# Moving the first head's projections into the last state-space group, and the first merge tiles' products and modulation terms into the last head

## What is computed

```python
hl = rms_norm(xl, g_pre_mix) * (1.0 + sc1_l) + sh1_l        # latent; hc the same for the context
z, xbc, dtr, q, f, i, og, gm, gh = split(h @ w_in)          # one input projection
xbc = silu(dwconv_centred(xbc, conv_w, conv_b))
y  = ssd_scan(...) + xs * d_skip                            # state-space branch: 4 groups of 8 heads, 2 directions
o  = gla_scan(silu(q), k(f), i, log_f)                      # gated linear attention (HGRN2): 8 heads, 2 directions
ys = rms_norm(ys * silu(z), g_ssm_norm)
oh = rms_norm(oh, g_hg_norm) * silu(og)
mixed = sigmoid(gm) * (ys @ w_branch_ssm) + sigmoid(gh) * (oh @ w_branch_hg)
xl = xl + gt1_l * rms_norm(mixed @ w_out, g_post_mix)
hl = rms_norm(xl, g_pre_ffn) * (1.0 + sc2_l) + sh2_l        # mod = silu(c) @ w_ada + b_ada gives sh, sc, gt
xl = xl + gt2_l * rms_norm(hier_moe(hl), g_post_ffn)        # 32 experts, top 2 inside the top group
```

## Time and profile before

| | us |
|---|---|
| median of 3 runs | 2322.83 (2321.36 to 2323.81) |
| the profiled execution, its own time | 2327.91 |
| its span | 2326.1 |
| PE busy | 1916.5 (82%) |
| DVE busy | 829.7 (36%) |
| ACT busy | 512.8 (22%) |
| POOL busy | 360.4 (15%) |

### The profile page before, as it was taken

How to read it: one execution, slowest core, us unless ns; L and a number is a source line. 1 busy time by engine, 2 the same in 40 slices (tenths; PEclk the granted TensorE clock), 3 DMA queues, 4 the chain that set the end, 5 groups by cost and what they waited for, 6 DMA issues and landing times.

```text
span 2326.1 us, 20169 instructions
## 1 busy us (share of the span) xinstructions
PE 1916.5 (82%) x7320; PEld 1043.9 (45%) x7320; DVE 829.7 (36%) x1438; ACT 512.8 (22%) x781; POOL 360.4 (15%) x400
## 2 busy tenths in 40 slices
PE   6888888888885898899988679999964977778773
PEld 2454544544543566666656544444442333333321
DVE  1444354444456065554566442212232000000003
ACT  2221231231322144433244320000240000000002
POOL 1011011021020144323444310000000100000000
PEclk9898898998996899999999799999976999999996
DMA  6113113103111211111110136242336999999993
GB/s 242 40 36 95 44 33 91 45 27 99 36 37 36 81 46 36 36 36 36 36 45 9 45 143 209 94 150 81 112 139 267 428 430 430 429 429 429 429 418 134
DMA packets 153549, 350.16 MB, mean 151 GB/s; under 512 B 14066, under 2 KB 104395, under 8 KB 140443
## 3 DMA queue, kind: packets, MB, share of 16 engines
q1 hardware_dynamic: 144282, 332.68, 37.9%
q10 hardware_dynamic: 4176, 8.41, 1.0%
q0 software_dynamic: 5040, 8.40, 1.0%
HBM read 346.09 MB, written 13.32 MB: 155 GB/s over the span
## 4 chain that ended last, share of the span: by engine, by line
PE 59%; DMA 17%; DVE 9%; issue 7%; ACT 6%; POOL 2%; SPq 1%; DVEq 0%; ACTq 0%; POOLq 0%
PE bank L575 11%; PE bank L1066 7%; PE bank L1045 5%; PE bank L1865 5%; DMA arena<-in_w_up_dram 4%; PE bank L1386 4%; PE bank L629 4%; PE bank L1071 3%; DMA arena<-in_w_down_dram 3%; DMA arena<-in_w_gate_dram 3%; PE bank L1405 2%; PE bank L647 2%; PE bank L1883 2%; PE bank L1390 2%; PE bank L1104 2%
## 5 line engine op out<-in xcount | busy, mean ns | idle before, releaser
L575 PE MATMUL bank<-stay,arena 128*128 128x512 f32 (+1 forms) x704 | 253.9, 521 | 24.8 <-DVE arena L732 22.6
L1865 PE MATMUL bank<-arena 128*64 128x512 f32 x832 | 201.8, 642 | 52.5 <-DMA arena<-in_w_up_dram 33.3
L575 PEld LDWEIGHTS bank<-stay,arena 128*128 128x128 f32 x704 | 140.6, 201 | 143.3 <-issue 117.9
L1066 PE MATMUL bank<-arena 128*128 128x512 f32 x384 | 180.4, 625 | 20.0 <-ACT arena L973 15.8
L1865 PEld LDWEIGHTS bank<-arena 128*64 128x64 f32 x832 | 70.4, 148 | 182.3 <-issue 179.1
L1927 DVE TENSOR_TENSOR arena<-arena,bank 128x512 f32<-128x512 f32 x17 | 11.7, 688 | 331.2 <-PE bank L1865 331.2
L1066 PEld LDWEIGHTS bank<-arena 128*128 128x128 f32 x384 | 76.5, 203 | 113.3 <-issue 91.5
L629 PE MATMUL bank<-arena,stay 128*128 128x512 f32 x256 | 120.9, 628 | 0.0
L1045 PE MATMUL bank<-stay,arena 128*128 128x512 f32 x256 | 116.1, 612 | 0.0
L1386 PE MATMUL bank<-stay,arena 128*128 128x512 f32 x256 | 111.2, 592 | 0.0
L1104 PE MATMUL bank<-arena 128*128 128x128 f32 x448 | 68.7, 306 | 49.1 <-DVE arena L1212 36.2
(11 more groups left out here) (370 smaller groups left out, 2838.4 us busy)
## 6 DMA issues: line engine op xcount, KB each, us to landing
arena<-in_w_gate_dram SPq DMA_DIRECT2D x26, 2048.0 KB, 26.4
arena<-in_w_up_dram SPq DMA_DIRECT2D x26, 2048.0 KB, 27.6
arena<-in_w_down_dram SPq DMA_DIRECT2D x24, 2048.0 KB, 27.0
arena<-in_w_in_dram SPq DMA_DIRECT2D x64, 512.0 KB, 4.0
arena<-in_w_ada_dram SPq DMA_DIRECT2D x12, 2048.0 KB, 10.1
stay<-in_w_down_dram SPq DMA_DIRECT2D x10, 2048.0 KB, 26.4
stay<-in_w_gate_dram SPq DMA_DIRECT2D x8, 2048.0 KB, 26.6
stay<-in_w_up_dram SPq DMA_DIRECT2D x8, 2048.0 KB, 27.4
```

What stands on the lines that cost most here:

```text
L575: mm = pe.matmul(ps[:, 0:n], w[:, k, :], hT[:, k, o:o + n], start=(k == 0), stop=(k == KT - 1))
L1066: mm = pe.matmul(b[:, :], w[:, k, :], src[:, k, 0:LAT], start=(k == 0), stop=(k == KT - 1))
L1865: mm = pe.matmul(b[cols, :], xgT[r][:, k, cols], w[u][:, k, :], start=(k == 0), stop=(k == KT - 1))
```

## The change

Three things are moved, and nothing is computed otherwise:

1. `unit` and `unit_copy` become `head_unit` and `head_unit_copy`, and head 0's eight units stand in the last group at the places where the other groups have `project`: units 0 and 1 at `j` = 8, 2 and 3 at 10, 4 at 12, 5 at `q` = 1, 6 at `q` = 3, 7 behind the last `q`. Their copies stand on ScalarE at `j` = 9, 11, 13, behind the z gate's SiLU, and behind the norm. The weights of head 0 are loaded behind the row of head 1 of the last group. The arena is laid out anew so that weights and projected values lie where nothing of the last group is alive.
2. In the last head, TensorE does the gate products of tiles 0 and 1 (copied out raw by `gate_copy`, their sigmoid taken in place later), and the state-space product of tile 0 in four quarters. What stays of tile 0 behind the head is the product with `ohT`; of tile 1 the two branch products.
3. The `w_ada` tile of tile 0 is loaded as soon as the head's units let go of `hTp`, and VectorE takes its eight operations in the last head, between the chunk states and the end of the head.

The mask wait of VectorE (`s_lev`) stands behind the first head's start. Other edits (one memset semaphore fewer, a shared one for the output norm, a strided home for the gates in `hT`) move nothing.

```diff
+        def early_gate(pe, j, b, half):
+            if not half:
+                if j:
+                    pe.wait_ge(s_wm[1], 32)
+                    pe.wait_ge(s_gc, b + 1)
+                else:
+                    pe.wait_ge(s_wg1, 32)
+                    pe.wait_ge(s_pev, START + 8 * HH - 1 + b)
+            for k in range(4 * half, 4 * half + 4):
+                mm = pe.matmul(bank[b][:, :], wmg[j][:, 8 * b + k, :], hT[:, k, 0:LAT], start=(k == 0), stop=(k == KT - 1))
+            if half:
+                mm.then_inc(s_gmp, 1)
+        def early_ssm(pe, quarter):
+            if not quarter:
+                pe.wait_ge(s_wm[0], 32)
+                pe.wait_ge(s_gc, 3)
+            for k in range(4 * quarter, 4 * quarter + 4):
+                pe.matmul(bank[0][:, :], wmb[0][:, k, :], ysT[:, k, :], start=(k == 0), stop=(k == 15))
...
+                    if last and j in (8, 10, 12):
+                        if j == 8:
+                            pe.wait_ge(s_hp, KT)
+                        for u in {8: (0, 1), 10: (2, 3), 12: (4,)}[j]:
+                            head_unit(pe, 0, u)
...
+                    if last and q in (1, 3):
+                        head_unit(pe, 0, 5 + q // 2)
...
+                else:
+                    head_unit(pe, 0, 7)
...
                 if not last:
                     for u in range(4):
-                        unit(h + 1, u)
+                        head_unit(pe, h + 1, u)
+                else:
+                    for b in range(2):
+                        for half in range(2):
+                            early_gate(pe, 0, b, half)
...
-                    if last and i in (0, 2):
-                        if i == 0:
-                            pe.wait_ge(s_pev, START + 8 * HH)
-                        pe.wait_ge(s_wm[0], 64)
-                        merge_gate(pe, i // 2, 0)
+                    if last and i == 0:
+                        early_gate(pe, 1, 0, 1)
+                    if last and i in (2, 3):
+                        early_gate(pe, 1, 1, i - 2)
+                    if last and i in (4, 5):
+                        early_ssm(pe, i - 4)
...
                 if not last:
-                    unit(h + 1, 7)
+                    head_unit(pe, h + 1, 7)
+                else:
+                    early_ssm(pe, 2)
                 pe.wait_ge(s_sqh, h + 1)
                 pe.matmul(bank[7][:, :], ones[:, :], sqb, start=True, stop=True).then_inc(s_sum, 1)
+                if last:
+                    early_ssm(pe, 3)
...
                 if not last:
                     start(h + 1)
                     sums(h + 1)
+                else:
+                    modulation_terms(dve, own, 0)
                 finish(h)
```

More of the change, by code:

```diff
@@ L521, in body @@
                         centre(g + 1, (j - 9) // 2, False)
+                    if last and j in (9, 11, 13):
+                        for u in {9: (0, 1), 11: (2, 3), 13: (4,)}[j]:
+                            head_unit_copy(act, 0, u)
                 act.wait_ge(s_zc, 4 * g + 4)
@@ L825, in ssd_vector @@
             body(G - 1, True)
-        at[0] = after_long
-        wh = [take(KT, P) for _ in range(5)]
+        at[0] = KT * LAT
         pf = [take(T) for _ in range(2)]
         pq, pog, pV = take(LAT), take(LAT), take(T)
+        Vh = take(NCH, P)
+        assert at[0] == after_long
+        wh = [take(KT, P) for _ in range(5)]
+        ohT = take(KT, LAT)
+        after_oh = at[0]
         lf = [take(T) for _ in range(2)]
@@ L851, in build @@
         lbh, omlh, ghg = take(2), take(2), take(1)
+        KD = [take(T) for _ in range(2)]
         NL = len(LEVELS)
@@ L1074, in hg_tensor @@
-            for u in range(8):
-                unit(0, u)
             def body(h, last):
```

268 lines of the change are left out of this document (159 added, 109 removed).

## The result

The changed kernel takes 2271.25 us in the median of 4 runs (2264.99 to 2273.61), the kernel before, on the same chip, 2323.32 (2321.36 to 2329.52): a ratio of 0.9767, 95% interval 0.9753 to 0.9781, or 54 us saved (51 to 57). The forecast was 56.0 us, 2266.8.

The account below looks back on a forecast made before the run. The closing expert-weight stream, DMA-bound, starts only after the second norm, so savings ahead of it count in full: 29.6 (units less masks) plus 26.4 (last head, merge tiles) gave 56.0 us, 2266.8 from 2322.83, range 2254 to 2284.

Parts of the forecast that it names:

- Units, 30.0 said: Last group: head 0's units cost 21.3 us there and free the 51.3 us they held alone, gaining 30.0.
- The rival by which the units hide nothing: Last group: inserted units lengthen each step, gain 3.8 us instead of 29.6, giving 2292.6; chance 0.06.
- Masks, 0.4 late said: Head 0's start: GpSimd's masks end at 795.2, its first head work is due at 794.8, so 0.4 us late.
- the rival's text: Masks beside VectorE's scans slowed 2.2 times, 13.4 us late, 2280.2; about 2 us called more probable; chance 0.06.
- the sign of being right: Head 0's start: the masks were to end within 1 us of the first scan.
- The last head, +4.3 said: Last head: gate and state-space pieces put into TensorE's queue end the head 4.3 us later.
- half a product (3.5): Last head, behind level 2: half a gate product on TensorE was put at 3.5 us.
- the rival of the pieces at the lower clock: Last head: six pieces between levels and behind outputs take 7 us, not 3.5; 21 us more, 2287.8; chance 0.08.
- Terms and merge tiles: Behind the last head: tiles 0 and 1 need 30.0 us instead of 60.7; modulation operations hidden in the head.
- The 26.4: Last head and merge tiles together: 30.7 us gained behind the head less 4.3 for its later end.
- The stream's length: End of program: the expert weights' stream does not depend on its start, so savings ahead arrive in full.
- The clock staying low through the merge tiles: Merge tiles: each loses 36 us at the lower clock, 2483 with all six; chance 0.02 of slower than before.

Follow-up runs that it names:

- units_alone: Changed kernel with head 0's eight units back in a row ahead of the loop over heads, weights still loaded early: 2292.75 us, ratio 0.985.
- masks_early: Changed kernel with head 0's level masks in a tensor of their own, made without waiting for the last group's transposes: 2272.85 us, ratio 0.9772.
- gaps_masks: Changed kernel with last-head pieces set into earlier gaps, tile 1's whole first gate ahead of level 0, and masks in their own tensor: 2256.19 us, ratio 0.9695.
- gaps_masks_2: The kernel of `gaps_masks` run once more, beside the same kernel without the masks' own tensor: 2260.77 us, ratio 0.9705.
- keep_busy: Changed kernel plus four matmuls that nobody needs behind level 1 of the last head: 2268.86 us, ratio 0.9762.
- ssm_behind: Changed kernel with all four quarters of tile 0's state-space product together behind the last head's sum of squares: 2273.67 us, ratio 0.9779.

## Why the prediction was right, and where it was off

The sum was 56.0 us. On the same chip the medians give 52.1 and the segments 52.2, which falls short by 0.6 in the units, 0.7 in the masks, 1.0 in the heads and 1.5 in the last head and the merge tiles.

**Units, 30.0 said, 29.4 found.** (The 29.6 of the prediction has the 0.4 us of the masks in it, which this segment, ending at the sigmoids, doesn't hold.) By the chunk state of step 8, and adding the 5.70 us of offset: the end of step 9's products was put at 721.6 and is 722.3; the steps' last product at 744.7, is 745.9 (740.16 in the trace); the last VectorE pair at 769.2, is 770.1; the transposes at 780, are 781.2. They are 0.7 to 1.2 us late, since the first pair of units takes 11.45 (702.54 to 713.99) where the group before had 10.83, and since the last steps keep 0.6 us of waits. That TensorE behind the transposes would lose its wait for weights was in the 51.3 already; `units_alone` prices it at 3.3. The rival by which the units hide nothing is out: undone, they cost 26 us in the segment and 20 in the median.

**Masks, 0.4 late said, about 1.1 found.** Two errors that partly cancel. The masks take 15.6 us, not 11.15, 4.4 us of stretch against the 2 that the rival's text held more probable, and end 5.1 us behind the first scan, where within 1 us was the sign of being right; GpSimd's first work for the head is 4.8 us late. Of it 1.1 reach level 1: the late L976 took 1.47 us instead of 2.75, with no scan beside it, while in the kernel before and in `masks_early` a scan ran beside it; and level 0 doesn't come later. The rival had the stretch right, and 13.4 us as its price, twelve times too much, as it took the whole lateness to lie on the chain.

**The heads, a term put at nothing, about 1 us.** Beside the masks' 1.1 they took 1.0 us more (489.1 - 1.1 against 487.0). It isn't scatter alone: `masks_early`, `gaps_masks` and `gaps_masks_2`, with the units in the last group and the masks out of the way, have 487.9, 488.0 and 487.9, while the three traces without units in the group have 487.0, 487.1 and 486.8. It enters in head 0: there the projection behind level 2 took 7.73 us in the kernel before (848.33, granted clock 0.90) and 8.72 in `masks_early` (820.35, 0.80), behind levels 1 and 2 at the same distance from the table load. Level 1 itself, behind a wait of 3.31 us in both, took 2.07 us before (clock 0.50) and 1.16 in `masks_early` (1.00). So the clock rises and falls at other moments of the head; why is not shown. (Behind head 0 the heads take 69.4 and 70.5 us in turn in both kernels, in opposite order, so that the lateness stands at every second head, the last one among them.)

**The last head, +4.3 said, +6.2 found.** Level 2 stands 36.8 us behind the head's start, 36.35 by the working. Level 6 ends 60.5 us behind it, 3.8 later than before instead of 1.5, and from there to the sum it is +2.4 where +2.8 was said. What was mis-sized is "half a product (3.5)" behind level 2: it took 5.70, 2.1 more, and TensorE had stood 4.11 us for VectorE ahead of that level. The working had granted the slow clock to the half behind level 0 only (up to 5.6, found 5.68). `keep_busy` shows it by undoing it: with the 4.11 us filled, 3.60. So the rival of the pieces at the lower clock holds for two of its six pieces, 4.2 us of its 21, of which 2.1 were in the sum. The size moves from execution to execution: `ssm_behind` and `masks_early`, with the same waits, have 4.60 and 5.16, and 4.72 and 5.22.

**Terms and merge tiles.** 30.0 us from the end of the head to tile 2 were said, and 29.8 found; tile 2 doesn't wait for its weights. The 26.4 were 24.9, the difference being the head's. Right in sum, but partly for a wrong reason: the gain was booked as products removed, and `ssm_behind` shows that the state-space product, 14 us of it, was worth 0.2 to 2 where it was put, being paid back as the longer head. Of the modulation terms the text said that they took 6.22 us alone and that without their cover they'd cost up to 6.2. The reading was wrong: the 6.22 us were a wait for `w_ada`, which the early load removes, and the place of the operations is worth 1.7, by way of a DMA. What is left to carry the rest of the gain is the gates that fill the 12.95 us ahead of level 0, and tile 0's that no longer stand between the levels; no run took these back alone, so their share is argued from the timeline and not shown by an experiment.

**The end.** The stream's length isn't seen to depend on when it starts: the scatter from 600.6 to 606.8 holds for both kernels, and all traces of 2252 to 2326 us lie in it. The clock staying low through the merge tiles didn't happen (14.00 for the 16 matmuls of tile 1).

## What to carry to other kernels

Where work is moved into the gaps of another stage, put each piece ahead of the wait that it is to fill, and none between the last product and the reduction that ends the stage: the same pieces in the same head gave 9.8 us more in the segment and 6.8 in the median by these two rules together. Read what the stage's other engines need next before filling a gap further; where VectorE sets the time of the next piece, an earlier TensorE only waits elsewhere (6.1 us sooner, 1.3 kept). And compare kernels by segments between events that both have, since the stream at the end scatters by as much as a small edit is worth; a segment too is read against a point ahead of the edit, as one trace was 1.8 us ahead there by luck.

## What was not expected of the hardware

GpSimd's selects of 64 columns take 0.24 to 0.66 us when VectorE is quiet, growing towards the last masks. Beside VectorE's scans of 1.78 and 1.75 us two of them took 1.58 and 2.12 us, where the same two took 0.44 and 0.66 before: three times as long and more. The Trainium skill's "GPSIMD Engine Reference", section 1 (Specifications), says that the two engines share an SBUF interface; the trace agrees, and gives the size. In the last head a piece of 3.60 us of TensorE's work took 5.68 and 5.70 (4.60 and 5.16 in another execution) where TensorE had stood 3.22 and 4.11 us ahead of the level before it, and 3.60 where it had stood 0.67: matmuls that nobody needs, put into a gap, shortened the head by 1.5 us.
